# Delta rule's preparation: the first level reads PSUM with its copy behind it, the upper mask is added in front of the exponential, the projection's low parts come later

## The reference

```python
diff = gc[..., :, None] - gc[..., None, :]
decay = jnp.where(tril, jnp.exp(jnp.where(tril, diff, 0.0)), 0.0)
lower = jnp.where(strict, jnp.einsum("bhnid,bhnjd->bhnij", k_beta, k) * decay, 0.0)
t_inv = lax.linalg.triangular_solve(eye + lower, jnp.broadcast_to(eye, lower.shape),
                                    left_side=True, lower=True, unit_diagonal=True)
attn = jnp.where(tril, jnp.einsum("bhnid,bhnjd->bhnij", q, k) * decay, 0.0)
...
v_new = u_i - jnp.einsum("bhcd,bhde->bhce", w_i, state)
o = (jnp.einsum("bhcd,bhde->bhce", q_i * jnp.exp(g_i)[..., None], state)
     + jnp.einsum("bhij,bhje->bhie", a_i, v_new))
```

## Time and profile before

| | |
|---|---|
| median of 3 runs | 2647.21 us (2646.25 to 2649.93) |
| time of the profiled execution | 2641.73 us |
| its span, first to last instruction | 2639.9 us |
| mean granted TensorE clock | 0.965 of full |
| delta stage | about 345 to 650 us of the span |

### The profile page before, as it was taken

How to read it: one execution, slowest core, us unless ns; L and a number is a source line. 1 busy time by engine, 2 the same in 40 slices (tenths; PEclk the granted TensorE clock), 3 DMA queues, 4 the chain that set the end, 5 groups by cost and what they waited for, 6 DMA issues and landing times.

```text
span 2639.9 us, 36732 instructions
## 1 busy us (share of the span) xinstructions
PE 2440.3 (92%) x12666; PEld 2029.3 (77%) x12666; DVE 1694.7 (64%) x3028; ACT 1105.4 (42%) x2029; POOL 916.7 (35%) x822
## 2 busy tenths in 40 slices
PE   7999999999999999997999999998888879999987
PEld 5888777778878887787999999766665668865566
DVE  5762245554479777774888766698888943245654
ACT  4432233333333234763566633443333343246643
POOL 4000033222200100014667665677787510124422
PEclk9999989999999999997999999999999879899999
DMA  4222211111222446994999999899999912531231
GB/s 179 96 91 92 87 49 49 49 49 73 96 88 85 144 144 235 397 365 136 348 333 335 335 359 345 287 388 387 386 387 387 369 64 96 163 96 57 60 136 48
DMA packets 190652, 519.52 MB, mean 197 GB/s; under 512 B 25824, under 2 KB 79200, under 8 KB 189632
## 3 DMA queue, kind: packets, MB, share of 16 engines
q1 hardware_dynamic: 139360, 351.95, 37.2%
q0 software_dynamic: 46560, 139.10, 14.7%
q10 hardware_dynamic: 4608, 26.92, 2.5%
HBM read 456.54 MB, written 56.62 MB: 194 GB/s over the span
## 4 chain that ended last, share of the span: by engine, by line
PE 68%; DVE 14%; DMA 7%; issue 5%; ACT 3%; POOL 1%; another core or an unknown queue 1%; SPq 0%; DVEq 0%; ACTq 0%
PE ps L2020 66%; DMA work<-gate_matrix 6%; DVE work L1789 4%; DVE look_lo L1649 2%; DVE up_lo L1816 1%; DVE act_lo L1822 1%; PE ps L2552 1%; DVE work L1811 1%; DMA work<-dram_stream,acts 1%; POOL work L753 1%; ACT work L1266 1%; ACT look_hi L1068 0%; PE ps L2195 0%; DVE ring_lo L1962 0%
## 5 line engine op out<-in xcount | busy, mean ns | idle before, releaser
L688 POOL DMA_INDIRECT work<-dram_stream,acts x256 | 338.9, 1324 | 456.9 <-PE ps L2020 243.4
L2020 PE MATMUL ps<-x_hi,down_hi 128*128 128x384 f32 (+1 forms) x1144 | 414.1, 362 | 11.0 <-DVE ring_lo L1642 6.5
L2020 PE MATMUL ps<-x_hi,ring_lo 128*128 128x384 f32 (+1 forms) x1152 | 410.0, 356 | 4.7 <-issue 4.7
L2020 PE MATMUL ps<-x_lo,down_hi 128*128 128x384 f32 (+1 forms) x1144 | 406.6, 355 | 4.3 <-issue 4.2
L1789 DVE SCALAR_TENSOR_TENSOR work<-work,acts 128x1024 f32<-128x1024 f32 x254 | 325.8, 1283 | 17.4 <-DMA work<-dram_stream,acts 8.8
L2020 PE MATMUL ps<-xn_lo,w_hi 128*128 128x512 f32 x752 | 297.6, 396 | 0.0
L2020 PE MATMUL ps<-xn_hi,w_hi 128*128 128x512 f32 x696 | 283.8, 408 | 10.1 <-ACT work L1221 4.5
L1030 ACT ACTIVATE down_hi<-ring 128x1024 fp32r<-128x1024 f32 x128 | 135.7, 1060 | 353.5 <-PE ps L2020 254.7
L2020 PE MATMUL ps<-xn_hi,ring_lo 128*128 128x512 f32 x712 | 282.6, 397 | 0.0
L2020 PE MATMUL ps<-work 128*128 128x128 f32 (+7 forms) x1912 | 266.1, 307 | 10.3 <-issue 5.5
L2020 PE MATMUL ps<-up_hi,act_hi 128*128 128x512 f32 x512 | 216.4, 423 | 60.6 <-DVE act_lo L1822 56.3
(11 more groups left out here) (409 smaller groups left out, 4692.6 us busy)
## 6 DMA issues: line engine op xcount, KB each, us to landing
ring<-dram_stream SPq DMA_DIRECT2D x529, 512.0 KB
hidden<-acts SPq DMA_DIRECT2D x128, 192.0 KB
gate_matrix<-work ACTq DMA_DIRECT2D x4, 4096.0 KB
work<-hidden SPq DMA_DIRECT2D x32, 512.0 KB
work<-gate_matrix SPq DMA_DIRECT2D x32, 512.0 KB
look_values<-acts ACTq DMA_DIRECT2D x24, 256.0 KB, 5.8
work<-dram_stream,acts POOLq DMA_INDIRECT x256
mix_gates<-work SPq DMA_DIRECT2D x16, 256.0 KB, 3.8
```

Source lines behind the costliest of these rows:

```text
L688: pool.indirect_dma_start(ROW[:, n % ROWS, :], None, up_rows, bass.IndirectOffsetOnAxis(ap=ROW_IDX[:, 1 - second, col:col + 1], axis=0))\
L2020: return nc.tensor.matmul(o, lhsT, rhs, start=start, stop=stop, skip_group_check=True)
```

## The change

The first level's product now reads PSUM (bank b + 2) directly as soon as `lt` is there, and the ScalarE copy `lts` of the same bank waits for that product (a new step `ltm`), so it stands behind it. The upper mask is no longer multiplied onto the exponential by GpSimd (`etm` is gone): a tile `NOT_YET`, 0 where the mask is 1 and -1e30 where it is 0, is made once and added to the minimum in front of the exponential. `z_low` of the round before moves from behind `diff` to behind `t1`. In the whole program VectorE has one instruction more, GpSimd eight fewer, TensorE and ScalarE the same number. The changed kernel's line numbers differ by one to three.

```diff
+        NOT_YET = view(work, 31400, P)
...
-        V_STEPS = ["vb", "gu", "bkk", "diff", "l", "tt", "t"]
+        V_STEPS = ["vb", "gu", "bkk", "diff", "l", "ltm", "tt", "t"]
...
-        dG = [Steps(sem(f"delta_pool_{p}"), [], ["mask", "lk1", "etm", "lk2", "kdec"] + [f"lk{l}" for l in range(3, LEVELS)])
+        dG = [Steps(sem(f"delta_pool_{p}"), [], ["mask", "lk1", "lk2", "kdec"] + [f"lk{l}" for l in range(3, LEVELS)])
...
-                def etm(p, h, s):
-                    pool.wait_ge(dA[p].sem, dA[p].done(r, "e"))
-                    g_.tensor_tensor(s.et, s.et, over(upper, 1, TT), ALU.mult).then_inc(dG[p].sem, 1)
...
-                    if l <= 2:
-                        each(etm if l == 1 else kdec)
+                    if l == 2:
+                        each(kdec)
...
                 def lts(p, h, s, b):
-                    act.wait_ge(dT[p].sem, dT[p].done(r, "lt"))
+                    act.wait_ge(dV[p].sem, dV[p].done(r, "ltm"))
                     nc.scalar.activation(four(s.df), ps[:, b + 2, :], ACT.Copy).then_inc(dA[p].sem, 1)
...
                     norm_qk(0)
+                    link(v.tensor_scalar(NOT_YET, upper, 1.0, 1e30, ALU.subtract, ALU.mult))
...
                     v.tensor_scalar(s.ed, s.df, 0.0, None, ALU.max)
-                    v.tensor_scalar(s.et, s.df, 0.0, None, ALU.min).then_inc(dV[p].sem, 1)
+                    v.scalar_tensor_tensor(s.et, s.df, 0.0, over(NOT_YET, 1, TT), ALU.min, ALU.add).then_inc(dV[p].sem, 1)
...
                 def upper_kq(p, h, s, b):
-                    dve.wait_ge(dG[p].sem, dG[p].done(r, "etm"))
                     dve.wait_ge(dT[p].sem, dT[p].done(r, "kq"))
                     v.tensor_tensor(s.et, bank(b + 1), s.et, ALU.mult).then_inc(dV[p].sem, 1)
 
                 def level0(p, h, s, b):
-                    dve.wait_ge(dA[p].sem, dA[p].done(r, "lts"))
-                    link(v.tensor_tensor(s.tt, s.df, over(const("block")[:, 0:P], 1, TT), ALU.mult))
+                    dve.wait_ge(dT[p].sem, dT[p].done(r, "lt"))
+                    v.tensor_tensor(s.tt, bank(b + 2), over(const("block")[:, 0:P], 1, TT), ALU.mult).then_inc(dV[p].sem, 1)
+                    dve.wait_ge(dV[p].sem, dV[p].done(r, "ltm"))
                     v.tensor_tensor(s.tt, over(ident, 1, TT), s.tt, ALU.subtract).then_inc(dV[p].sem, 1)
...
-                for fn, steps in ((vb, 2), (bkk, 1), (diff, 1), (lower, 1), (level0, 1),
+                for fn, steps in ((vb, 2), (bkk, 1), (diff, 1), (lower, 1), (level0, 2),
                                   (t1, 1)):
                     each(fn, steps)
-                    if r and fn is diff:
+                    if r and fn is t1:
                         z_low(r - 1)
```

## The result

| | before | changed |
|---|---|---|
| median | 2646.73 us (4 runs, 2643.52 to 2649.93) | 2623.35 us (4 runs, 2621.28 to 2633.11) |
| ratio, 95% interval | | 0.9927, 0.9900 to 0.9955 |
| profiled execution, its span | 2641.73, 2639.9 us | 2633.11, 2631.3 us |
| granted TensorE clock, mean | 0.965 | 0.969 |

The account below looks back on a forecast made before the run. TensorE, the busiest engine, was taken to lose time waiting on VectorE in the delta stage's preparation. Rounds 1 to 3 at 3.23 us (9.69) plus round 0's 2.09 gave 11.8 us: 2647.2 to 2635.4 us, range 2627.5 to 2642.

Parts of the forecast that it names:

- The second `t1`: Second head's transpose on TensorE in the delta stage: 3.23 us earlier in rounds 1 to 3, 2.09 in round 0.
- the fused instruction: VectorE's minimum with mask, before the exponential: 0.68 us instead of 0.42, so 0.26 more for each head.
- the product from PSUM: Level 0's product on VectorE: 0.68 us for work instead of 1.75, as GpSimd does not hold it up.
- the first subtraction: Level 0's subtraction for acts on VectorE: over when GpSimd begins, 0.69 us instead of 1.63, saving 0.94.
- the last one: Level 0's subtraction for work on VectorE: still meets GpSimd, 1.27 us instead of 1.64, saving 0.37.
- the lock's pattern: VectorE and GpSimd take turns, each waiting for the other's whole instruction; VectorE ends about 0.55 us behind GpSimd.
- `lk1` of work: GpSimd's level 1 instruction for the second head: held up by the last subtraction, about 1.7 us, still in time.
- The rival in which GpSimd also blocks the product from PSUM: Level 0: work's product takes 1.75 us again, 1.4 us lost a round, 2641.1 us; chance 0.11 shared with `lk1` in the way.
- the one in which `lk1` of work goes first: GpSimd takes it before the waiting subtraction: 1.3 us a round lost, 2640.6 us; chance 0.11 shared with the blocked product.
- the low stretch behind the preparation: TensorE at 1.2 GHz after each round's idle stretch; 15.6 us on the chain, 0.42 us lost per microsecond.
- the clock rival: TensorE's low stretches shrink or go with less idle time: up to 6.6 us more gain, 2628.8 us; chance 0.18.
- the waits for the second subtraction: TensorE's waits on VectorE's second subtraction of level 0: down from 13.5 us in all to about 6.

Follow-up runs that it names:

- `warm`: Kernel before, plus TensorE matmuls that nobody reads in its gaps of the preparation; ratio 0.9972, stage 286.14 us.
- `delay`: Changed kernel, plus 2.86 us of VectorE products that nobody reads ahead of level 0 in each round; ratio 1.0019, stage 291.91 us.
- `psum_only`: Kernel before with only the first product reading PSUM and the copy behind it; ratio 0.9939, on another chip 0.9949; stage 269.65 us.
- `no_mask`: Changed kernel without its mask part: minimum alone before the exponential, mask product back on GpSimd; ratio 0.9942, in a second run 0.9938.
- `mask_only`: Kernel before with only the mask added in front of the exponential and GpSimd's mask products removed; ratio 1.0014, stage 286.01 us.
- `after_again`: The changed kernel once more, unaltered, against the kernel before; ratio 0.9911, median 2620.83 us, stage 274.49 us.
- `after_third`: The changed kernel unaltered, a third comparison against the kernel before, on another chip; ratio 0.9936, median 2629.27 us, stage 271.71 us.
- `after`: The changed kernel in its first comparison against the kernel before; ratio 0.9927, median 2623.35 us, stage 270.70 us.
- `before`: The kernel before the change, in its first measurement; median 2646.73 us, stage 288.16 us.
- `before_again`: The kernel before, unaltered, compared against itself; ratio 0.9994, median 2641.95 us, stage 288.96 us.
- `zlow_only`: Kernel before with only `z_low` moved from behind the difference to behind `t1`; ratio 0.9981, stage 284.86 us.

## Why the prediction was wrong

**What held, step by step.** The second `t1` comes 3.19 us earlier in rounds 1 to 3 (forecast 3.23) and 2.05 in round 0 (2.09); in sum 11.63 against 11.8. Each price holds as well: the fused instruction took 0.68 to 0.69 (0.68 taken), the product from PSUM 0.68 for both heads, the first subtraction 0.69, the last one 1.28 to 1.29 (1.27 from the lock's pattern), `lk1` of work 1.64 (about 1.7). The lock pattern read from the earlier trace rows thus gave the price of an overlap that the trace of before did not contain. The rival in which GpSimd also blocks the product from PSUM is out, and so is the one in which `lk1` of work goes first. The Trainium skill has the rule that, of VectorE's instructions without a perf mode, only those with two SBUF inputs ask for the port pair shared with GpSimd ("SBUF — State Buffer", section "SBUF: two separate sides"). The trace agrees: L1520, one input from PSUM, kept its 0.68 us where GpSimd's L647 began beside it. The Trainium skill's figure of 120 cycles from PSUM against 58 from SBUF ("VectorE: DVE Perf Modes", section "The TRN2 errata") would have made the product dearer by an estimated 0.065 us; the trace shows 0.68 for L1520 and 0.68 for L1512, so nothing was rightly put for it.

**The step that failed: TensorE's clock.** The sum counted the low stretch behind the preparation as unchanged, and the clock rival got a chance of 0.18. It was the case that came. Its price was right: 6.6 us forecast, 6.16 measured in level 1 (6.8 against the second execution of before), and `warm` gives 6.15 with nothing else changed. What failed was the reading of the evidence against it, that TensorE "still waits there more than it works". Over the whole preparation that was not so even before. Round 1 of before, then of the changed kernel (columns as above):

```profile
433.76:445.71 11.95, 7.24 (x89) 4.88 (x88) 10.91 (x16) 4.54 (x12) 5.73 (x4) 0.86 0.32 114
431.11:439.87 8.76, 6.43 (x90) 4.51 (x88) 7.87 (x14) 4.54 (x12) 1.85 (x2) 1.00 0.11 31
```

TensorE stood idle for 4.7 of 11.95 us before and for 2.3 of 8.76 after, half of the old idle time. The longest waits had been 2.2 and 1.8 us, each right in front of a `t1`; in the changed kernel the same two are 0.7 and 0.2, with transposes and fill matmuls between them. The forecast knew that the waits for the second subtraction would fall from 13.5 to about 6 us (they fell to 3.5) and yet left the clock, which had fallen after the first or the second of these waits, out of the sum. The Trainium skill's general rule that idle gaps between bursts of matmuls drop the clock ("TensorE: Matmul & The Clock Gate", section "HAM oscillation") stood for the rival. `warm` and `delay` agree with it here: level 1 takes 7.12 us at 1.00 and up to 8.80 at 0.73. With the clock's term the sum is 11.8 + 6.6 = 18.4, the stage shows 17.46. One more reading was wrong: before does show half clock beyond level 1, for 3.4 us late in round 1 (last section).

**The range.** Even the rival's 2628.8 lies above the median of 2623.35. 17.46 us out of 2646.7 would be a ratio of 0.9934. The three comparisons, 0.9927, 0.9911 and 0.9936, have it inside their intervals, and the kernel before alone ranges over 24 us on one chip. The range of the forecast had a microsecond on either side of the rival and nothing for this. One place of the spread can be seen: from the start of the last low part of the expert layer's `look` phase (L1649 before, L1647 changed) to that of the expert weights (L1642 before, L1640 changed) 492.0 and 495.3 us passed in the two profiles of before, and 500.1, 491.5 and 493.3 in the three of the changed kernel. The 500.1 belong to the profiled execution of the result: up to 1150 us its work stands 16.8 us ahead of before, behind this phase 8.7. Whether the further 6 us of the median's 23.4 are more than spread stays open. The profiled executions show no gain behind the stage: from its end to the end of the kernel 1994.0 and 1998.2 us pass before, 2002.3, 1992.1 and 1997.6 in the changed kernel.

**The parts.** The forecast gave `etm` nothing and `z_low` about 0.1 us a round. For `etm` that holds in the new order: in `psum_only` and `no_mask` it begins after the last subtraction. For `z_low` no run has the changed kernel with `z_low` in its old place, so the 0.1 us is not shown. On their own the two free 0.4 us in three rounds and 1.15 us in three: with the old order `etm` held the last subtraction, and `z_low`, by holding the first `lt`, the whole chain from copy to product. With the product from PSUM and `etm` still on GpSimd, `z_low` left in place costs 8.89 - 8.21 = 0.68 us a round. The mask costs 0.54 in the changed kernel, the 0.52 forecast, and buys nothing there. The stage was shortened by the product from PSUM: alone it takes 18.5 us off, all three together 17.5.

**`NOT_YET`** was hidden: 0.22 us in front of a wait of VectorE for TensorE's transposes, which ends at 358.32 (0.91 us of idle remain).

## What to carry to other kernels

Where a trace shows a lower TensorE clock right behind a wait that the change shortens, the clock belongs in the sum with its price, the time of the same matmuls at either level, and the question is what keeps it down once the wait is short. Two instructions that take turns at the SBUF ports show it in their ends; one operand in PSUM takes an instruction out of the game, and moving the copy behind the reader costs nothing where the copy's own reader is late. Whether a wait lets the clock fall cannot be told from its length alone, as the rounds of `mask_only` show. Parts of a change that pay alone may pay nothing together: here one of three carried all of it.

## What was not expected of the hardware

Another low stretch shows late in the rest of a round, where the scan over the chunks runs. Below are windows of round 0, first in the second execution of the changed kernel (`after_again`), then in the first. The first execution reaches the same matmuls 3.04 us later, so its windows are shifted by that; they cover the same work up to the fall.

```profile
404.00:408.00 4.00, 3.80 (x30) 3.42 (x29) 2.37 (x8) 2.29 (x8) 0.00 (x0) 1.00 0.00 0
406.00:410.00 4.00, 3.93 (x32) 3.50 (x30) 2.30 (x7) 1.83 (x7) 0.00 (x0) 0.99 0.00 0
408.00:412.00 4.00, 3.66 (x22) 3.24 (x23) 0.98 (x3) 0.98 (x6) 0.00 (x0) 0.74 0.01 2
412.00:416.00 4.00, 4.00 (x22) 4.00 (x20) 1.95 (x6) 1.64 (x4) 0.00 (x0) 0.50 0.00 0
416.00:420.00 4.00, 3.94 (x16) 3.35 (x17) 0.83 (x3) 0.85 (x5) 0.00 (x0) 0.50 0.00 0
```

```profile
407.04:411.04 4.00, 3.79 (x30) 3.41 (x29) 2.37 (x8) 2.29 (x8) 0.00 (x0) 1.00 0.00 0
409.04:413.04 4.00, 3.93 (x32) 3.50 (x30) 2.30 (x7) 1.83 (x7) 0.00 (x0) 1.00 0.00 0
411.04:415.04 4.00, 3.62 (x27) 3.07 (x28) 1.54 (x5) 1.28 (x7) 0.00 (x0) 1.00 0.01 2
```

The same program with the same work holds 1.00 in one execution and falls to 0.50, 1.2 GHz, in the other, for 10.2 us, which costs 3.6 us. In the 4 us up to the fall TensorE had been busy for 3.93 us, and for the same 3.93 where it did not fall, so idle time does not tell the two apart.

Before has such a stretch too, but a short one, in round 1 of both its executions:

```profile
493.60:497.00 3.40, 3.40 (x28) 2.40 (x30) 1.87 (x7) 2.47 (x13) 0.00 (x0) 0.50 0.00 0
```

Short ones of 3.4 us also lie in round 2 of `mask_only`, round 2 of `after_third` and round 0 of `delay`; these rests take 48.9 to 49.6 us instead of 48.4 to 48.7. The long ones, 10 to 14 us, make a rest 3.6 to 4.6 us longer. They come 7 times in 27 rounds (rounds 0 to 2 of nine profiles) in the kernels in which the clock of level 1 had changed in all rounds: `after`, `warm`, `delay`, `psum_only`, `no_mask` and their repeats. In `before`, `before_again`, `mask_only` and `zlow_only` they come never, in 12. So few rounds, several of them from one execution, do not show that the higher clock of level 1 brings them, and what starts them was not found. In those nine profiles they take back on average about 1 us a round, and the ratios of the changed kernel have them in it.
